# Differential attention in two groups of heads, with value and output projection pieces between its units

## The chip, the cores and the metric

The kernel runs on one core of a Trainium2 chip. A core has five engines with a queue each: TensorE (PE; its weight loads are shown apart as PEld), VectorE (DVE), ScalarE (ACT), GpSimd (POOL, not used here) and SyncE (SP, which here only issues transfers). The metric is the device time of one launch in microseconds. Lower is better.

## What is computed

Two transformer blocks of 2 layers each over 256 tokens of width 1024, all in float32. Each layer is a gated feed-forward, a mixer and a second gated feed-forward. Layer 1 of the first block has the mixer that the change touches, differential attention:

```python
def diff_attention_mixer(h, w_in, w_out, qk_g, lam_p, subln_g, cos, sin, lambda_init):
    q, k, v = jnp.split(h @ w_in, 3, axis=-1)          # 8 heads, 2 maps of 64 each; v: 8 heads of 128
    q = partial_rope(rmsnorm(q, qk_g[0]), cos, sin)
    k = partial_rope(rmsnorm(k, qk_g[1]), cos, sin)
    lam = exp(sum(lp[0] * lp[1])) - exp(sum(lp[2] * lp[3])) + lambda_init
    ...                                                # per block of 128 queries, causal keys
        p = jax.nn.softmax(jnp.where(mask, sc, -jnp.inf), axis=-1)
        a = p[:, :, 0] - lam * p[:, :, 1]
        outs.append(jnp.einsum('bhqk,bhkv->bhqv', a, v[:, :, :s1]))
    o = rmsnorm(concatenate(outs), subln_g) * (1.0 - lambda_init)
    return o.transpose(0, 2, 1, 3).reshape(Bn, S, D_MODEL) @ w_out
```

## The kernel before

Every engine's instruction stream is written out by hand, with semaphores between them, so the order of each queue is the order of the source. A weight matrix is streamed in pieces of 128 by 2048 floats through a ring of three buffers. SP loads a piece into `raw` as soon as DVE has released the buffer. ACT rounds it to `wH` (`cut`, L514), DVE subtracts to get `wL` (`cut`, L897), and PE multiplies three times for each product (`times_three`, L1599, L1601 and L1603) so that the sum has float32 accuracy. ACT may cut piece n once PE has eaten piece n-3. A piece of 512 output columns and half of the depth takes 24 multiplications, 12 for each of the two tiles of 128 tokens.

The mixer uses 16 pieces: two each for six chunks of 512 columns (chunks 0 and 1 queries, 2 and 3 keys, 4 and 5 values), then four for the output projection. Products go to four PSUM banks `PY` (the first two are `PA`, the last two `PB`) and two banks `GU` in turn; `TM` takes transposes. For chunks 0 to 3 ACT squares the bank (L751), DVE normalizes and rotates, PE transposes (`turn_chunk`) and ACT copies the result to `qT` or `kT` (L757). The two value chunks are copied to `vB` by ACT (L665). Ahead of all this DVE works out lambda and the angles (`lambda_and_angles`, L1255 to L1275) in front of the cut of the first piece of the loop.

Attention then runs in 8 units of two heads and one tile of 128 queries; units 0 to 3 are tile 0 (128 keys, "small" below), units 4 to 7 tile 1 (256 keys, "large"). For unit u:

- PE `scores(u)` (L1909) into `PB` for even u and `PA` for odd u, so the scores of u+2 are issued ahead of the rest of unit u;
- DVE `mask_and_max(u)` (L1282), ACT `exponentials(u)` (L733), DVE `difference(u)` (L1293 to L1302). DVE's queue holds mask(u+1) ahead of difference(u);
- PE `turn_weights(u)` (L1918), ACT `weights_out(u)` (L739), PE attention times values into `GU` (L1948; "AV" below).

After units 3 and 7, `out_norm` normalizes all 8 heads of one tile (ACT square L656 and root L660, DVE L1099 to L1104, then a second DVE pass, L1541, with the norm weight). Only after unit 7 does PE transpose the whole result (L1957) into `PY`, ACT and DVE split it in four banks (L728, L1248), and PE runs the four projection pieces. The third kind of mixer (`nsa`, layers 2 and 3) has units of its own through the same `scores` and `mask_and_max`, with one pair of banks and a whole piece in each unit; there DVE's queue holds the weights of unit u (`gated`) ahead of mask(u+1).

Of the kernel before, what the change touches and what calls it, by code (L numbers as in the profile page):

```python
# [25 lines left out]
P = 128  # L26
S = 256
# [38 lines left out]
N_LATE = 6  # L66
# [9 lines left out]
PIECES_B = whole([h * 512 for h in range(6)]) + whole([3 * D + h * 512 for h in range(2)])  # L76
# [39 lines left out]
def build(nc, T, out, upto=99):  # L116

    with ExitStack() as ctx:
# [34 lines left out]
        vec = sb("vec", [P, P + 4 * MODS + 64])  # L153
        cols, bT, peT = vec[:, 0:P], vec[:, P:P + 4 * MODS], vec[:, P + 4 * MODS:]
# [87 lines left out]
        PBf = PY[:, 2:4, :].rearrange("p b n -> p (b n)")  # L242
        TMf = TM[:, :, :].rearrange("p b n -> p (b n)")
# [66 lines left out]
        s_sv = sem("s_sv")  # L310
        s_yb = sem("s_yb")
# [37 lines left out]
        def _(sp):  # L349
# [81 lines left out]
            def late_constants():  # L431
# [3 lines left out]
                for to, name in ((vb[:, :], "a_onorm"), (vb2[:, 0:P], "b_qk_g"), (vb2[:, P:2 * P], "b_subln"),  # L435
# [70 lines left out]
        def _(act):  # L506
# [218 lines left out]
            def high_bank(b):  # L725

                act.wait_ge(s_ot, t.next(s_ot))
                act.activation(xH2[:, b, :], PY[:, b, :], ACT.Copy).then_inc(s_xh, 1)  # L728
# [12 lines left out]
            def diff():  # L741
# [6 lines left out]
                for c in range(4):  # L748
                    banks = GUf if c % 2 == 0 else PAf
                    act.wait_ge(s_eaten, t.next("done", 2))  # L750
                    act.activation(sq_, banks, ACT.Square).then_inc(s_sq, 1)  # L751
# [4 lines left out]
                    dst = (qT if c < 2 else kT)[:, 4 * (c % 2):4 * (c % 2) + 4, :].rearrange("p h s -> p (h s)")  # L756
                    act.activation(dst, TMf, ACT.Copy).then_inc(s_aT, 1)  # L757
                evacuate(vB[:, :, 0:512], GU[:, :, :])
                cut()
                exponentials(0, P)  # L760
                evacuate(vB[:, :, 512:D], PY[:, 0:2, :])
                cut()
                for u in range(8):
                    if u < 7:
                        exponentials(u + 1, P * ((u + 1) // 4 + 1))
                    weights_out(u, S * (u // 4 + 1))
# [5 lines left out]
                for b in range(4):  # L772
                    high_bank(b)
                cut()
                cut()
# [109 lines left out]
        def _(dve):  # L885
# [164 lines left out]
            def ffn(l, j):  # L1050
# [25 lines left out]
                loop(NF - 3, turns > 0)  # L1076
                gate_columns(l, j)
# [18 lines left out]
            def head_norm(src, groups, width, spread, sq):  # L1096
# [7 lines left out]
                chained(dve.tensor_tensor(spread, src, bc(st8[:, 3, 0:groups].unsqueeze(2), [P, groups, width]),  # L1104
                                          ALU.mult))
# [140 lines left out]
            def low_bank(b):  # L1246
                dve.wait_ge(s_xh, t.next(s_xh))
                dve.tensor_tensor(xL2[:, b, :], PY[:, b, :], xH2[:, b, :], ALU.subtract).then_inc(s_xl, 1)  # L1248

            def lambda_and_angles():  # L1250
# [6 lines left out]
                chained(dve.tensor_scalar(vb2[:, P:2 * P], vb2[:, P:2 * P], 1.0 - LAMBDA_INIT, None, ALU.mult))  # L1257
# [14 lines left out]
                dve.tensor_scalar(flat, flat, -3.1415925, 3.1415925, ALU.max, ALU.min).then_inc(s_trig, 1)  # L1272
                dve.wait_ge(s_trigd, 1)
# [3 lines left out]
            def mask_and_max(u, tile, banks):  # L1277

                dve.wait_ge(s_score, t.next(s_score))
                src, dst, width = banks.rearrange("p (m s) -> p m s", s=S), p_[u % 2], P * (tile + 1)  # L1280
                for m in range(4):
                    ins = dve.tensor_tensor_reduce(dst[:, m, 0:width], src[:, m, 0:width],  # L1282
# [33 lines left out]
            def diff():  # L1316
                lambda_and_angles()
                cut()
                q16 = qk_.rearrange("p (g n) -> p g n", n=64)
                q4 = qk_.rearrange("p (t g n) -> p t g n", t=NT, n=64)  # L1320
                shape = [P, NT, 8, 8]
                for c in range(4):
                    banks = GUf if c % 2 == 0 else PAf
# [892 lines left out]
```

## Time and profile before

| | |
|---|---|
| median of 3 runs | 2291.11 us (2289.98 to 2291.81) |
| profiled execution, own time | 2292.84 us |
| its span in the profile | 2291.1 us |
| PE busy | 2181.4 us, 95% of the span |
| DVE busy | 1627.5 us, 71% |
| ACT busy | 1062.4 us, 46% |
| mean granted clock of PE | 0.985 |

The span is the time from the first to the last recorded instruction; busy times are sums of instruction durations. A PE multiplication's own duration includes the time to drain, so the distance from one start to the next is the better price of one in a run.

### The profile page before, as it was taken

Reading aid. Unit: us, or ns where it says so; the run is one execution under the profiler, and the core shown is the slowest. Engines: PE = TensorE matmul, PEld = TensorE weight load, DVE = VectorE, ACT = ScalarE, POOL = GpSimd, SP = SyncE. Lnnn points to the kernel's source line nnn. Section 1 sums busy time; section 2 is a strip of 40 time slices with the busy share of each in tenths; the row PEclk is TensorE's granted clock in tenths of the full one; section 3 lists DMA queues with packets and bytes.
Section 4 is the critical chain, followed back from the end, with each engine's and each line's share of the span. In section 5 each row is a group of like instructions: output and inputs, shape, how many; then the busy total and the mean of one; then the engine's idle time right before and its main releaser. Section 6 shows DMA issues by size and latency. Waiting matters only on the chain.

```text
span 2291.1 us, 29525 instructions
## 1 busy us (share of the span) xinstructions
PE 2181.4 (95%) x10588; PEld 1803.3 (79%) x10588; DVE 1627.5 (71%) x2262; ACT 1062.4 (46%) x1265; POOL 0.2 (0%) x4
## 2 busy tenths in 40 slices
PE   3999989999999996999999999999999999999998
PEld 2888987788788874788788887778878888777887
DVE  6777767777777786677677766577767776656545
ACT  3344533443534455533443446653344344665334
POOL 0000000000000000000000000000000000000000
PEclk9999999999999997999999999999999999999999
DMA  7898524688688641498678853359867885334553
GB/s 308 315 336 318 214 85 153 233 316 312 230 326 315 225 171 59 162 336 299 217 277 310 317 211 129 131 186 341 296 216 282 307 316 212 129 129 147 191 194 129
DMA packets 128372, 537.25 MB, mean 234 GB/s; under 512 B 15040, under 2 KB 15904, under 8 KB 109344
## 3 DMA queue, kind: packets, MB, share of 16 engines
q1 hardware_dynamic: 128288, 536.12, 64.5%
q8 instruction: 55, 0.90, 0.2%
q14 instruction: 29, 0.24, 0.0%
HBM read 534.96 MB, written 1.10 MB: 234 GB/s over the span
## 4 chain that ended last, share of the span: by engine, by line
PE 86%; DVE 8%; ACT 4%; DMA 1%; issue 1%; SPq 0%; DVEq 0%; ACTq 0%
PE GU L1599 14%; PE GU L1603 14%; PE GU L1601 14%; PE PY L1599 11%; PE PY L1601 11%; PE PY L1603 11%; DVE wL L897 3%; PE TM L1643 1%; ACT wH L514 1%; ACT M L566 1%; PE PY L2006 1%; ACT xH L561 1%; PE PY L1909 1%; DMA M<-in_ada_t 1%; PE TM L1799 1%
## 5 line engine op out<-in xcount | busy, mean ns | idle before, releaser
L897 DVE TENSOR_TENSOR wL<-raw,wH 128x2048 fp32r<-128x2048 f32 x344 | 776.7, 2278 | 231.7 <-ACT wH L514 230.6
L514 ACT ACTIVATE wH<-raw 128x2048 fp32r<-128x2048 f32 x344 | 645.3, 1900 | 156.9 <-PE PY L1603 93.2
L1599 PE MATMUL GU<-wH,xH 128*128 128x512 f32 (+1 forms) x1584 | 627.6, 396 | 34.2 <-DVE xL L1021 30.7
L1603 PE MATMUL GU<-wH,xL 128*128 128x512 f32 (+1 forms) x1584 | 616.1, 389 | 0.0
L1601 PE MATMUL GU<-wL,xH 128*128 128x512 f32 (+1 forms) x1584 | 615.0, 388 | 0.0
L1599 PEld LDWEIGHTS GU<-wH,xH 128*128 128x128 f32 x1584 | 298.2, 188 | 100.4 <-issue 27.6
L1603 PEld LDWEIGHTS GU<-wH,xL 128*128 128x128 f32 x1584 | 297.9, 188 | 62.7
L1601 PEld LDWEIGHTS GU<-wL,xH 128*128 128x128 f32 x1584 | 298.5, 188 | 57.1
L594 ACT ACTIVATE hH<-TM 128x512 fp32r<-128x512 f32 x80 | 47.9, 599 | 592.2 <-PE TM L1643 592.2
L910 DVE CUSTOM_DVE_ANT_0 ada<-ada,cond 128x1024 f32<-128x1024 f32 x272 | 316.7, 1221 | 0.0
L1599 PE MATMUL PY<-wH,hH 128*128 128x512 f32 x640 | 198.6, 392 | 0.9 <-DVE wL L897 0.9
L1034 DVE TENSOR_TENSOR hL<-TM,hH 128x512 fp32r<-128x512 f32 x80 | 55.3, 692 | 200.0 <-ACT hH L594 199.4
L1601 PE MATMUL PY<-wL,hH 128*128 128x512 f32 x640 | 197.2, 389 | 0.0
L1603 PE MATMUL PY<-wH,hL 128*128 128x512 f32 x640 | 197.1, 389 | 0.0
L1599 PE MATMUL PY<-wH,xH 128*128 128x512 f32 x448 | 182.1, 406 | 9.4 <-ACT ada L842 3.0
L1601 PE MATMUL PY<-wL,xH 128*128 128x512 f32 x448 | 177.1, 395 | 0.0
L1603 PE MATMUL PY<-wH,xL 128*128 128x512 f32 x448 | 176.7, 394 | 0.0
L1599 PEld LDWEIGHTS PY<-wH,hH 128*128 128x128 f32 x640 | 119.0, 188 | 27.3 <-DVE wL L897 3.4
L1601 PEld LDWEIGHTS PY<-wL,hH 128*128 128x128 f32 x640 | 120.1, 188 | 25.2
L1603 PEld LDWEIGHTS PY<-wH,hL 128*128 128x128 f32 x640 | 120.1, 188 | 25.1
L1599 PEld LDWEIGHTS PY<-wH,xH 128*128 128x128 f32 x448 | 85.7, 191 | 30.0 <-DVE wL L897 4.3
L1603 PEld LDWEIGHTS PY<-wH,xL 128*128 128x128 f32 x448 | 85.6, 191 | 18.9
(282 smaller groups left out, 1899.8 us busy)
## 6 DMA issues: line engine op xcount, KB each, us to landing
raw<-in_up_w SPq DMA_DIRECT2D x352, 512.0 KB, 6.0
ada<-in_ada_t SPq DMA_DIRECT2D x136, 1024.0 KB, 7.8
raw<-in_down_w SPq DMA_DIRECT2D x176, 512.0 KB, 4.7
raw<-in_c_w SPq DMA_DIRECT2D x96, 512.0 KB, 4.3
raw<-in_a_w SPq DMA_DIRECT2D x40, 512.0 KB, 4.4
raw<-in_b_w SPq DMA_DIRECT2D x32, 512.0 KB, 4.3
M<-in_ada_t SPq DMA_DIRECT2D x8, 1024.0 KB, 12.4
gB<-gates SPq DMA_DIRECT2D x12, 512.0 KB, 5.8
```

Source lines behind the costliest of these rows:

```text
L514: act.activation(wH[:, to, 0:words], raw[:, slot, 0:words], ACT.Copy).then_inc(s_high, 1)
L561: act.activation(xH[:, 2 * b:2 * b + 2, toks], modf[:, i, 2 * b:2 * b + 2, :], ACT.Copy).then_inc(s_xh, 1)
L566: ins = act.activation(modf[:, i, d, :], PT[:, i, d, :], ACT.Identity, bias=mod[:, m + d:m + d + 1], scale=scl[:, d:d + 1])
L594: act.activation(hH[:, :, :].rearrange("p f s -> p (f s)"), TM[:, 0, :], ACT.Copy).then_inc(s_hh, 1)
L897: dve.tensor_tensor(wL[:, to, 0:words], raw[:, slot, 0:words], wH[:, to, 0:words], ALU.subtract).then_inc(s_split, 1)
L910: ins = dve.tensor_tensor_reduce(w, w, cond[:, :], 1.0, 0.0, ALU.mult, ALU.add, acc[:, 2 * q + b:2 * q + b + 1])
L1034: dve.tensor_tensor(hL[:, :, :].rearrange("p f s -> p (f s)"), TM[:, 0, :], hH[:, :, :].rearrange("p f s -> p (f s)"), ALU.subtract).then_ ...
L1599: pe.matmul(outs[i], aH, wh[i], start=first, stop=False)
L1601: pe.matmul(outs[i], aH, wl[i], start=False, stop=False)
L1603: ins = pe.matmul(outs[i], aL, wh[i], start=False, stop=last)
L1643: ins = pe.transpose(TM[:, 0, f * S + i * P:f * S + (i + 1) * P], sh[:, 1, i, f * P:(f + 1) * P], ident)
L1799: ins = pe.matmul(dst[:, h, :], kk[:, h, :], qq[:, h, :], start=True, stop=True)
```

## The change

The mixer is reordered.

1. The pieces come as chunks q 0-3, k 0-3, q 4-7, k 4-7, v, v. The units take heads 0 to 3 first (units 0 to 3), then heads 4 to 7; tile 0 and tile 1 alternate. Unit 0's scores are issued between the two pieces of the first value chunk.
2. The second value chunk has no place of its own ahead of the units: units 0 to 3 each hold 12 multiplications of 256 columns, units 4 and 5 hold 24 of them each.
3. All scores go to `PB` alone. `scores(u+1)` is issued at the head of unit u, behind AV of unit u-1.
4. `out_norm` works on a group of four heads for both tiles. Its multiplication with the norm weight is gone: the weight, as a column, is the scale of ACT's and DVE's split. Group 0 is copied out of `GU` by ACT first. Unit 6 holds the transposes of group 0, unit 7 the first projection piece; the second follows unit 7; then come the transposes of group 1 and the last two pieces.
5. `lambda_and_angles` moves into the feed-forward before the mixer, behind its loop. What needs the exponentials (`lambda_last`) stays, behind the cut.
6. One constant fewer is loaded late, and the table of columns is 16 columns wider.

```diff
-PIECES_B = whole([h * 512 for h in range(6)]) + whole([3 * D + h * 512 for h in range(2)])
+PIECES_B = whole([h * 512 for h in (0, 2, 1, 3, 4, 5)]) + [
+    (k0, 3 * D + h * 512, 512) for k0 in (0, 4) for h in range(2)]
...
+            def high_group(grp):
                 act.wait_ge(s_ot, t.next(s_ot))
+                act.activation(xH[:, 4 * grp:4 * grp + 4, :].rearrange("p (b d) s -> p b (d s)", d=2),
+                               TM[:, :, :] if grp else PAb, ACT.Identity, scale=subln).then_inc(s_xh, 1)
...
             def diff():   # ACT
                     cut()
                     cut()
+                    if c == 3:
+                        exponentials(0, P)
                     act.wait_ge(s_ot, t.next(s_ot))
...
                 evacuate(vB[:, :, 0:512], GU[:, :, :])
                 cut()
-                exponentials(0, P)
-                evacuate(vB[:, :, 512:D], PY[:, 0:2, :])
-                cut()
                 for u in range(8):
                     if u == 4:
                         head_norm(GUf, xn[:, 0, :])
+                        act.activation(on_[0], GUf, ACT.Copy).then_inc(s_readA, 1)
+                    if u < 7:
+                        exponentials(u + 1, P * ((u + 1) % 2 + 1))
+                    weights_out(u, S * (u % 2 + 1))
+                    if u == 3:
+                        act.wait_ge(s_half, 1)
+                        act.activation(vB[:, :, 512:768], PAb[:, :, 0:256], ACT.Copy).then_inc(s_readA, 1)
+                    if u == 4:
                         head_root(8)
+                    if u == 5:
+                        evacuate(vB[:, :, 768:D], PAb[:, :, 256:512])
+                        cut()
+                    if u == 6:
+                        high_group(0)
+                        cut()
+                root_table()
                 head_norm(GUf, xn[:, 0, :])
                 head_root(8)
+                cut()
+                high_group(1)
...
             def diff():   # DVE
-                lambda_and_angles()
-                cut()
+                cut()
+                lambda_last()
...
                 for u in range(8):
                     if u < 7:
                         if u:
                             dve.wait_ge(s_a, t.next(s_a))
-                        mask_and_max(u + 1, (u + 1) // 4, PBf if u % 2 else PAf)
-                    difference(u, u // 4)
+                        mask_and_max(u + 1, (u + 1) % 2, PBb)
+                    difference(u, u % 2)
                     if u == 0:
                         cut()
                     if u == 4:
                         out_norm(0)
+                    if u == 5:
+                        cut()
+                    if u == 6:
+                        low_group(0)
+                        cut()
                 out_norm(1)
+                cut()
+                low_group(1)
...
             def diff():   # PE
                 for u in range(8):
+                    tile, first = u % 2, 4 * (u // 4)
+                    if u < 7:
+                        following(u + 1)
+                    if u == 0:
+                        pe.wait_ge(s_aT, t.next(s_aT))
                     turn_weights(u, tile, 2)
+                    if u < 4:
+                        ...
+                        ins = value_half(0, u // 2, u % 2)
+                    elif u < 6:
+                        ...
+                        value_half(1, u - 4, 0)
+                        value_half(1, u - 4, 1).then_inc(s_eaten, 1)
+                    elif u == 6:
+                        pe.wait_ge(s_readA, t.next(s_readA))
+                        pe.wait_ge(s_on, t.next(s_on))
+                        for h in range(4):
+                            for i in range(NT):
+                                ins = pe.transpose(...)
+                        ins.then_inc(s_ot, 1)
+                    else:
+                        pe.wait_ge(s_scored, t.next(s_scored))
+                        pe.wait_ge(s_xl, t.next(s_xl))
+                        project(0, 0)
                     pe.wait_ge(s_aT, t.next(s_aT))
                     ...
+                project(0, 1)
+                pe.wait_ge(s_on, t.next(s_on))
+                ...
+                project_last(1)
```

`value_half(part, q, i)` multiplies tile i with columns 256*part to 256*part+255 of the second value chunk over half q of the depth, 12 multiplications into `PA`.

## Rows read from the trace of the kernel before

**Rows 1.** The page, granted clock of PE in 40 equal slices, tenths of full speed.
```profile
PEclk9999999999999997999999999999999999999999
```
**Rows 2.** Windows: length, busy (count) of PE, PEld, DVE, ACT, POOL; clock; DMA; GB/s.
```profile
862.00:868.80 6.80, 6.80 (x35) 5.04 (x33) 2.25 (x10) 1.77 (x9) 0.00 (x0) 1.00 0.53 192
868.80:921.80 53.00, 30.15 (x145) 22.61 (x144) 35.66 (x126) 29.20 (x78) 0.00 (x0) 0.65 0.06 20
921.80:943.90 22.10, 22.07 (x98) 18.30 (x99) 11.59 (x13) 8.43 (x10) 0.00 (x0) 1.00 0.67 242
```
**Rows 3.** Windows, stretches of the units and of the tail behind them.
```profile
882.90:889.80 6.90, 4.44 (x30) 2.85 (x29) 6.30 (x30) 4.85 (x18) 0.00 (x0) 1.00 0.01 2
889.80:893.20 3.40, 0.43 (x4) 0.19 (x2) 1.36 (x2) 2.79 (x3) 0.00 (x0) 1.00 0.00 0
893.20:910.20 17.00, 12.33 (x50) 9.98 (x51) 11.38 (x40) 7.37 (x21) 0.00 (x0) 0.50 0.00 1
...
917.00:920.50 3.50, 3.42 (x16) 3.02 (x15) 1.65 (x3) 1.84 (x4) 0.00 (x0) 0.50 0.00 0
```
**Rows 4.** Timeline around the first chunks: start, duration, engine, line, operation, count [idle before].
```profile
804.75 0.50 PE L1599 MATMUL PY<-wH,xH 128*128 128x512 f32 x1
...
813.16 0.50 PE L1599 MATMUL PY<-wH,xH 128*128 128x512 f32 x1 [2.64 <-DVE wL L897]
...
820.37 1.03 PE L1974 MATMUL TM<-cst,M 128*128 128x128 f32 x8
...
833.22 0.48 PE L1599 MATMUL PY<-wH,xH 128*128 128x512 f32 x1
...
844.22 1.03 PE L1974 MATMUL TM<-cst,M 128*128 128x128 f32 x8
...
853.32 4.49 DVE L897 TENSOR_TENSOR wL<-raw,wH 128x2048 fp32r<-128x2048 f32 x2
```
**Rows 5.** Timeline, links of the units: L1282 mask, L1918 transposes, L1948 AV, L1909 scores.
```profile
875.47 0.28 DVE L1282 CUSTOM_DVE_ANT_0 M<-PY,cst 128x128 f32<-128x128 f32 x1
...
878.17 0.69 PE L1918 MATMUL TM<-cst,M 128*128 128x128 f32 x2 [1.23 <-DVE M L1302]
...
882.72 0.42 DVE L1282 CUSTOM_DVE_ANT_0 M<-PY,cst 128x256 f32<-128x256 f32 x1 [1.93 <-PE PY L1909]
...
883.59 0.71 PE L1948 MATMUL GU<-M 128*128 128x128 f32 x4 [0.47 <-ACT M L739]
...
884.24 1.13 PE L1909 MATMUL PY<-M 64*128 64x256 f32 x8
...
885.93 0.43 DVE L1282 CUSTOM_DVE_ANT_0 M<-PY,cst 128x256 f32<-128x256 f32 x1
...
885.95 0.44 PE L1918 MATMUL TM<-cst,M 128*128 128x128 f32 x2 [0.58 <-DVE M L1302]
...
889.57 0.66 PE L1918 MATMUL TM<-cst,M 128*128 128x128 f32 x4 [0.93 <-DVE M L1302]
```
**Rows 6.** Timeline, AV of a large unit and the scores behind it.
```profile
895.08 2.08 PE L1948 MATMUL GU<-M 128*128 128x128 f32 x8 [4.85 <-DVEq L1540]
...
897.09 2.08 PE L1909 MATMUL PY<-M 64*128 64x256 f32 x8
```
**Rows 7.** Timeline, small scores in the third mixer's units.
```profile
1427.46 0.72 PE L1909 MATMUL PY<-M 64*128 64x128 f32 x8
```
**Rows 8.** Chain of work: start, duration, a multiplication of 256 columns in the first mixer.
```profile
250.10 0.12 PE PY L1760
```
**Rows 9.** The page, cuts of a piece: shapes, count, busy, mean ns, idle before.
```profile
L897 DVE TENSOR_TENSOR wL<-raw,wH 128x2048 fp32r<-128x2048 f32 x344 | 776.7, 2278 | 231.7 <-ACT wH L514 230.6
L514 ACT ACTIVATE wH<-raw 128x2048 fp32r<-128x2048 f32 x344 | 645.3, 1900 | 156.9 <-PE PY L1603 93.2
```
**Rows 10.** Timeline, a copy of two banks (ACT) and a norm's multiplication (DVE).
```profile
868.86 1.02 ACT L665 ACTIVATE M<-PY 128x1024 f32<-128x1024 f32 x1 [2.83 <-PE PY L1603]
...
893.75 1.23 DVE L1104 TENSOR_TENSOR M<-GU,st 128x1024 f32<-128x1024 f32 x1
```

More of the change, by code:

```diff
@@ L748, in diff @@
                 for c in range(4):
-                    banks = GUf if c % 2 == 0 else PAf
                     act.wait_ge(s_eaten, t.next("done", 2))
-                    act.activation(sq_, banks, ACT.Square).then_inc(s_sq, 1)
+                    act.activation(sq_.rearrange("p (b n) -> p b n", b=2), PAb if c % 2 else GU[:, :, :],
+                                   ACT.Square).then_inc(s_sq, 1)
                     head_root(16)
@@ L1076, in ffn @@
                 loop(NF - 3, turns > 0)
+                if (l, j) == (1, 0):
+                    lambda_and_angles()
                 gate_columns(l, j)
@@ L1336, in diff @@
                 t.next(s_ot)
-                cut()
-                mask_and_max(0, 0, PBf)
+                mask_and_max(0, 0, PBb)
                 for u in range(8):
@@ L1348, in diff @@
                         out_norm(0)
+                    if u == 5:
[3 more added lines that the diff above has]
+                        cut()
                 out_norm(1)
-                for b in range(4):
-                    low_bank(b)
+                cut()
+                low_group(1)
                 t.next(s_at, 2)
-                t.next(s_ot, 4)
+                t.next(s_ot, 2)
                 t.next(s_on, 6)
-                t.next(s_readA, 2)
-                cut()
-                cut()
+                t.next(s_readA)
             def keys_rotated(src, branch):
@@ L1899, in hgrn, with scores @@
                 project_last(1)
-            def scores(u, tile, keys, heads, queries=qT, double=True):
-                banks = (PAf if double and u % 2 else PBf).rearrange("p (m s) -> p m s", s=S)
-                if u > double:
+            def scores(u, tile, keys, heads, queries, banks):
+                if u:
                     pe.wait_ge(s_scored, t.next(s_scored))
@@ L1924, in diff @@
                 keys = lambda h: kT[:, h, :]
-                heads = lambda u: (2 * (u % 4), 2 * (u % 4) + 1)
-                for c in range(1, 6):
+                heads = lambda u: (u // 2 * 2, u // 2 * 2 + 1)
+                following = lambda u: scores(u, u % 2, keys, heads(u), qT, PBb)
+                for c in range(1, 5):
                     if c > 1:
@@ L1929, in diff @@
                     for q in range(2):
-                        if c == 5 and q == 1:
-                            pe.wait_ge(s_aT, t.next(s_aT))
-                            scores(0, 0, keys, heads(0))
+                        if c == 4 and q == 1:
+                            following(0)
                         by_token(B if c % 2 else A, q)
                     turn_chunk(c - 1)
-                pe.wait_ge(s_readA, t.next(s_readA, 2))
-                scores(1, 0, keys, heads(1))
-                for u in range(8):
-                    tile = u // 4
-                    if u < 6:
-                        scores(u + 2, (u + 2) // 4, keys, heads(u + 2))
+                slots = [t.next("piece") % RING for _ in range(2)]
@@ new lines, in value_half @@
+                def value_half(part, q, i):
+                    cols_v = slice(part * S, (part + 1) * S)
+                    for k in range(4):
+                        d = 4 * q + k
+                        a, b = slice(i * P, (i + 1) * P), slice(k * 512 + part * S, k * 512 + (part + 1) * S)
+                        ins = times_three([B[i][:, cols_v]], xH[:, d, a], xL[:, d, a], [wH[:, slots[q], b]],
+                                          [wL[:, slots[q], b]], d == 0, d == ND - 1)
+                    return ins
@@ L1951, in diff @@
                         ins.then_inc(s_o, 1)
[L1952 to L1955 removed]
+                project(0, 1)
+                pe.wait_ge(s_on, t.next(s_on))
+                for h in range(4):
                     for i in range(NT):
[L1957 to L1963 removed]
+                        ins = pe.transpose(TMf[:, h * S + i * P:h * S + (i + 1) * P],
+                                           on_[1][:, i * 512 + h * P:i * 512 + (h + 1) * P], ident)
+                ins.then_inc(s_ot, 1)
+                pe.wait_ge(s_xl, t.next(s_xl))
+                project_last(1)
             def turn_chunk(c):
@@ L2042, in nsa @@
                 pairs = lambda u: (u // 2 % 2 * 2, u // 2 % 2 * 2 + 1)
-                following = lambda u: scores(u, u // 4, keys(u), pairs(u), qT2, False)
+                following = lambda u: scores(u, u // 4, keys(u), pairs(u), qT2, PY[:, 2:4, :])
                 following(0)
```

102 lines of the change are left out of this document (53 added, 49 removed).

## The prediction

> **What bounds the kernel now.** I read the page first, then windows by stage, then the timeline of the mixer with its waits. PE is busy 95% of the span, and the granted clock has one dent of note, in the slice of this mixer [rows 1]. The windows show why: the mixer's projections before and behind attention run PE without a gap at full clock, but the 53.0 us of attention between them keep it busy for 30.15 us at a mean clock of 0.65 [rows 2]. There PE waits in turn for DVE and ACT: the units are a chain through three engines, not a PE load. A second, smaller hole lies ahead: before the second piece of chunk 1 PE stands 2.64 us because DVE cuts that piece only behind lambda and the angles [rows 4]. So there are two things to win: the hole, and work of PE put into attention's idle time.
>
> **How the clock goes.** In the units the clock stayed at full speed for 882.9 to 889.8 with PE busy 4.44 of 6.90 us, was at half behind the 3.40 us with 0.43 us of work, stayed at half through 17.00 us in which PE was busy for 12.33 with short gaps, and came back only behind 3.42 of 3.50 us without a gap [rows 3]. At half, large scores take 2.08 us against 1.13, AV of a large unit 2.01 from start to start [rows 5, 6]; I take a factor of 1.93 for PE's work.
>
> **Part 1, lambda and angles moved.** The first chunk behind the hole took 820.37 - 804.75 = 15.62 us to its transposes, an undisturbed one 844.22 - 833.22 = 11.00 [rows 4]. The difference, 4.6 us, is the wait and the half-clock stretch that it caused; it goes. In the feed-forward the same small operations take 3.9 us of DVE (an estimate from the timeline: they fill DVE from the end of the cut before 804.75 on). A turn of that loop has three cuts of 2.28 us [rows 9] and lasts about 17 us of PE, so DVE has the room; the tightest piece I find is ready with it, and I charge 0 to 0.5 us, and take 0. Next late is PE's own load: the transposes of chunk 0 then wait for nothing. Gain 4.6, bounds 4.1 and 4.6.
>
> **Part 2, the unit's chain.** This is the term that decides. Before, scores(u+2) are in the other banks ahead of time, and DVE goes from one unit to the next without a pause (mask 882.72, next mask 885.93 [rows 5]). Now scores(u+1) wait for the AV of unit u-1, and in DVE's queue mask(u+1) stands ahead of difference(u). So transposes(u) need difference(u), which needs mask(u+1), which needs scores(u+1): one line, with PE idle for all of DVE's part. The links at full clock:
> - scores to mask start: 1.13 + 0.1 = 1.2 large [rows 5], 0.72 + 0.1 = 0.8 small [rows 7];
> - mask start to transposes: 878.17 - 875.47 = 2.70 small behind small, 885.95 - 882.72 = 3.23 large mask and small difference, 889.57 - 885.93 = 3.64 both large [rows 5]; a small mask and large difference is 2.70 + 3.64 - 3.23 = 3.1;
> - transposes 0.3 (small) or 0.6 (large) to the next start [rows 5]; 12 multiplications of 256 columns at 0.12 = 1.44 [rows 8];
> - AV 884.24 - 883.59 = 0.65 small [rows 5], half of 2.01 = 1.0 large [rows 6].
>
> ACT's copy of the weights hides under the 1.44 us. A small unit is 1.2 + 3.2 + 0.3 + 1.44 + 0.65 = 6.8 us, a large one 0.8 + 3.1 + 0.6 + 1.44 + 1.0 = 6.95.
>
> The 96 multiplications of 256 columns replace 48 of 512 at 0.227: 11.5 us for 10.9, a loss of 0.6 that is inside these terms. The Trainium skill ("TensorE: Matmul & The Clock Gate", LDWEIGHTS) prices a load of 128 columns at 107 ns, as long as 256 columns stream; were it not hidden, the 96 would cost some 10 us more by an estimate from that page. The row shows 0.12 us with a load for each, so it is hidden, and the sum is unchanged.
>
> **Part 3, the schedule at full clock**, in times of the trace before:
> - chunk 3's transposes start 11.8 behind 844.22, less 4.6, plus 0.7 of scores(0): 852.1, ended at 853.1 [rows 4]. Mask(0) stands behind two cuts, which end at 857.8 - 4.6 = 853.2 [rows 4]. Scores(1) start at 854.2.
> - Unit 0: DVE is done at 858.6, transposes and values at 860.4. But ACT has exponentials(0) (1.7), two copies of 1.0 [rows 10], a cut of 1.9 [rows 9] and exponentials(1) (2.0) ahead of the weights: AV(0) ends at 862.9.
> - Units 1 to 3: 6.95 + 6.8 + 6.95: 883.6.
> - Unit 4: as a small unit but 2.88 of values: 8.25, 891.9; ACT's square and copy and DVE's norm hide under it. Unit 5: 8.4, 900.3.
> - Unit 6 is the first pile-up. ACT copies the last values only when unit 5's piece is eaten, then cuts (0.6 + 1.9); DVE's cut of that piece (2.2) stands ahead of mask(7). Mask starts at 899.3 + 4.9 = 904.2, transposes(6) at 907.4; eight more transposes and AV: 909.2.
> - Unit 7 is the second: high half 1.0, cut 1.9, DVE's cut 2.2 and difference(7) 2.0 stand in one line behind the transposes of group 0 (908.6): 916.0. Then 0.6, a piece of 5.45, AV 1.0: 923.1.
> - Tail: square, sums, root, multiplication are 1.0 + 1.4 + 0.3 + 1.5, less than the piece beside them (928.5); transposes 0.9, high 1.2, low 1.3 (both of two banks): 931.9, and 10.9 for the last pieces: 942.8.
>
> Before, the last projection ends at 943.9 [rows 2]. So at full clock everywhere the change gives 1.1 us, with the 4.6 of part 1 in it. What the two moved value pieces and two moved output pieces save (21.8 us) is paid back by a chain 26 us longer. The second DVE pass of the norm (1.23, as [rows 10]) and the last wait for four separate banks are gone in these figures.
>
> **Part 4, the clock.** In a unit PE works 3.6 us and then stands 3.2 to 3.4 in one piece; in the pile-ups 6 us. That is nearer to the stretch of rows 3 behind which the clock was at half than to 4.44 of 6.90. The unbroken runs are 3.6 us, 7 at half, so it will also come back. PE's work on the chain from 853 to 932, without the two output pieces, is 8 scores and AV (12.9), transposes (5.3) and values (11.5) = 29.7 us. All at half adds 0.93 x 29.7 = 27.6; none adds 0. Of the 53 us before, about 70% were at half [rows 2]; in the third mixer's units, filled by whole pieces, none [rows 1]. I take half: +13.8. "A second HAM failure mode: psum-queue depth-cycling" on the same page of the Trainium skill describes such gaps as making the clock go back and forth; by that rule too the moved work would not be had at full rate, and the trace agrees (0.65).
>
> **Sum.** -1.1 + 13.8 = +12.7 on the profiled execution's 2292.84: 2305.5. That execution lies 1.7 us over the median shown, so 2303.8; I say 2304. What follows is the same feed-forward with the same transfers, whose buffers come free earlier; at nothing.
>
> **Rivals.**
> - *The clock holds.* The pieces between the units keep it at full, as in the third mixer. For it: 882.9 to 889.8 held with 64% busy. Against: there the gaps were short, and here each unit has one over 3 us, as the third mixer (weights of unit u ahead of mask(u+1)) has not. Time: 2291.1 - 1.1 + 0 to 3 = 2291.5. Chance 0.12.
> - *Faster: DVE does not hold up the last units.* If the cuts beside units 5 to 7 were through before mask(7) and difference(7) are due, the first pile-up gives back 4.7 us (mask at 901.5 less the wait) and the second 6, and with them 4 us of clock: 2304 - 15 = 2289. It needs ACT's cut of piece 13 to be ended by 899; the source has it behind the copy of the last values. Chance 0.05.
> - *Clock at half for nearly all of it*, as behind 893.2 [rows 3]: -1.1 + 25 = 2315. Against: the runs of 5.8 us at half in each unit have no gap, those of rows 3 had. Chance 0.10.
> - *The change does less than it says:* lambda's block delays the feed-forward's cuts by its 3.9 us and the gain of part 1 is lost: forecast + 4 = 2308. Chance 0.05.
>
> **Numbers.** The forecast as sized holds 0.68. A measurement of this kernel tells 0.2%, 4.6 us, from no change. Slower by more: forecast, half clock, lost gain and little of the first rival, 0.82. Within: most of the first rival and the low edge of the forecast, 0.11. Faster: 0.07. The range runs from 2291 (clock holds) to 2312 (three quarters at half, 2304 + 7).
>
> **What would show it.** Right: the hole before 813 is gone and the first transposes come 4.6 us earlier; scores of unit u+1 begin only behind AV of u-1; PE waits some 3.2 us for DVE's difference in each unit, a period of about 7 us at full and 10 at half clock; waits near 6 us before the transposes of units 6 and 7 that end in DVE's difference behind a cut; clock under 1 in about half of 853 to 932; last projection near 956. Wrong: transposes that wait for nothing (then DVE's queue isn't the link), a clock of 1.00 through the units, or time lost outside this mixer.

## The result, and the profile after

The changed kernel takes 2307.28 us (median of 4 runs, 2306.09 to 2308.90), the kernel before 2291.03 (4 runs, 2289.98 to 2291.81): a ratio of 1.0069 with a 95% interval of 1.0057 to 1.0082. The change makes the kernel 16 us slower. Its profiled execution took 2306.38 us with a span of 2304.6, which is 13.5 us over the 2292.84 of before's; the readings below say where those 13.5 lie. The other 2.7 come from how far each profiled execution lies from its own median: before's 1.8 us above, the changed one's 0.9 below.

The page of the changed kernel, in 40 slices of 57.6 us. PEclk is the granted clock in tenths:

```profile
PE   3999989999999995899999999999999999999998
...
PEclk9999999999999997899999999999999999999999
```

The dent of [rows 1] is still one slice, with a shallow second one behind it, and PE's load has its dent there (5 and 8 tenths). The loss is in this mixer. The start of a stage can be read from the first projection that waits for its normed input. In the timeline of PE, first in the kernel before, the start of this mixer:

```profile
791.03 0.47 PE L1599 MATMUL GU<-wH,xH 128*128 128x512 f32 x1 [1.43 <-DVE xL L1021]
```

and the same in the changed kernel:

```profile
792.89 0.47 PE L1627 MATMUL GU<-wH,xH 128*128 128x512 f32 x1 [1.43 <-DVE xL L1036]
```

The same row at the other boundaries gives a table of stage lengths, in us, from one such row to the next. It is used for every kernel below, each from its profiled execution:

| kernel | feed-forward ahead (1,0) | this mixer | feed-forward behind (1,2) |
|---|---|---|---|
| before | 191.93 | 156.08 | 193.02 |
| changed | 193.68 | 166.42 | 192.88 |

So 10.3 us were lost in the mixer and 1.8 in the feed-forward ahead of it, to which lambda's block has moved. That is 12.1 of the 13.5; the other 1.4 lie behind 1140 us, in code that is the same in both.

PE's waits in the kernel before from 790 to 945 (us in total, times, longest) are a mixed list. Its first lines:

```profile
PE PY L1957 <- DVE M L1541: 5.8, 1, 5.8
PE TM L1918 <- DVE M L1302: 5.8, 5, 2.3
PE GU L1948 <- DVEq L1540: 4.9, 1, 4.9
PE GU L1948 <- ACT M L739: 4.0, 7, 0.7
```

In the changed kernel, from 850 to 965, one line stands out:

```profile
PE TM L1944 <- DVE M L1324: 32.3, 8, 6.4
PE PY L1627 <- DVE xL L1265: 2.5, 1, 2.5
```

One wait, in each of the eight units: the transposes of the weights (L1944) for the difference (L1324). The same in the timeline, with units 1, 2, 3, 6 and 7 and the idle time before each in brackets:

```profile
869.08 1.11 PE L1944 MATMUL TM<-cst,M 128*128 128x128 f32 x4 [3.27 <-DVE M L1324]
878.02 0.44 PE L1944 MATMUL TM<-cst,M 128*128 128x128 f32 x2 [3.39 <-DVE M L1324]
885.55 0.66 PE L1944 MATMUL TM<-cst,M 128*128 128x128 f32 x4 [3.26 <-DVE M L1324]
...
915.10 0.69 PE L1944 MATMUL TM<-cst,M 128*128 128x128 f32 x2 [5.95 <-DVE M L1324]
924.75 1.11 PE L1944 MATMUL TM<-cst,M 128*128 128x128 f32 x4 [6.39 <-DVE M L1324]
943.31 0.50 PE L1627 MATMUL PY<-wH,xH 128*128 128x512 f32 x1 [2.52 <-DVE xL L1265]
```

There are two sizes of gap: 3.3 us in a plain unit, 6 us in the last two. The two transposes of a small unit take 0.44 us in some units and 0.69 in others, which is the clock. The windows of the changed kernel (columns: us, then busy time of PE, PEld, DVE, ACT and POOL, the granted clock, the DMA share and GB/s), first units 0 to 6, then two stretches at half clock, the second of which reaches into unit 7:

```profile
855.70:923.50 67.80, 36.65 (x220) 32.70 (x220) 32.48 (x118) 32.09 (x84) 0.00 (x0) 0.77 0.15 54
...
858.80:865.60 6.80, 5.28 (x26) 4.81 (x26) 3.50 (x6) 4.59 (x11) 0.00 (x0) 0.50 0.26 74
...
913.40:930.50 17.10, 9.00 (x30) 7.64 (x31) 6.93 (x15) 7.46 (x14) 0.00 (x0) 0.50 0.42 150
```

Against [rows 2], PE has more work in this part (the moved value and output pieces), and no engine is busy for more than 55% of it.

The time at half clock is not what changed. In both kernels it adds up to 40.9 us of the mixer: before in three stretches (814.7 to 818.1 behind the hole, 872.7 to 882.9, 893.2 to 920.5), in the changed kernel in seven (six between 858.8 and 930.5, and 944.1 to 947.5). PE is busy for 27.5 us of it before and for 30.8 in the changed kernel.

### The profile page after: what moved, and what is told of

Read it like the earlier page. It is cut to its first block, busy times and chain, and to the rows that moved or that the text cites. A ratio compares the mean times of both kernels' runs of the same rounds, so it can differ in the third digit from the quotient of the medians.

```text
span 2304.6 us, 29619 instructions
## 1 busy us (share of the span) xinstructions
PE 2184.7 (95%) x10636; PEld 1811.2 (79%) x10636; DVE 1624.0 (70%) x2258; ACT 1063.7 (46%) x1266; POOL 0.2 (0%) x4
## 4 chain that ended last, share of the span: by engine, by line
PE 86%; DVE 8%; ACT 3%; DMA 1%; issue 1%; SPq 0%; DVEq 0%; ACTq 0%
PE GU L1627 14%; PE GU L1631 14%; PE GU L1629 14%; PE PY L1627 11%; PE PY L1629 11%; PE PY L1631 11%; DVE wL L912 3%; PE TM L1671 1%; ACT wH L518 1%; PE PY L2066 1%; PE PY L1935 1%; ACT M L570 1%; ACT xH L565 1%; DMA M<-in_ada_t 1%; PE PY L1638 1%
## 5 line engine op out<-in xcount | busy, mean ns | idle before, releaser
L1627 PEld LDWEIGHTS GU<-wH,xH 128*128 128x128 f32 x1584 | 298.2, 188 | 100.4 <-issue 27.4
L1627 PE MATMUL PY<-wH,xH 128*128 128x512 f32 (+1 forms) x464 | 189.8, 409 | 7.9 <-ACT ada L857 3.0
L1629 PE MATMUL PY<-wL,xH 128*128 128x512 f32 (+1 forms) x464 | 184.0, 397 | 0.0
L1631 PE MATMUL PY<-wH,xL 128*128 128x512 f32 (+1 forms) x464 | 183.5, 396 | 0.0
L1627 PEld LDWEIGHTS PY<-wH,hH 128*128 128x128 f32 x640 | 118.9, 188 | 27.5 <-DVE wL L912 3.3
L1627 PEld LDWEIGHTS PY<-wH,xH 128*128 128x128 f32 x464 | 92.4, 199 | 27.6 <-issue 4.2
L1631 PEld LDWEIGHTS PY<-wH,xL 128*128 128x128 f32 x464 | 92.3, 199 | 18.7
```

Of the source, the lines that this page charges most:

```text
L1627: pe.matmul(outs[i], aH, wh[i], start=first, stop=False)
L1629: pe.matmul(outs[i], aH, wl[i], start=False, stop=False)
L1631: ins = pe.matmul(outs[i], aL, wh[i], start=False, stop=last)
```

## The experiments

Twelve kernels ran, in four groups (e1 to e4, e5 to e8, e9 to e11, e12), each group on one chip with the kernel before beside it (medians there 2291.5, 2291.9, 2290.9 and 2290.9). The changed kernel's 2307.28 comes from a run of its own, so differences of medians against it are across groups. The ratio is worked out from the single executions and not from the two medians. The stage lengths are those of one execution each; that of e7 lies 3.0 us above e7's median, e8's 2.5, e11's 1.8, e4's 1.6, the others' within 1.3. Where an expectation speaks of filler matmuls of 256 columns, they were in fact of 512, about 0.24 us each: the operand `xH[:, 4:6, :]` has 2 x 256 columns.

| run | median us | ratio to before (95%) | feed-forward ahead | mixer |
|---|---|---|---|---|
| e1 block in the feed-forward, late | 2291.85 | 1.0002 (0.9994 to 1.0011) | 196.49 | 151.21 |
| e2 block ahead of its loop | 2292.94 | 1.0000 (0.9991 to 1.0009) | 194.49 | 151.20 |
| e3 changed + fillers | 2296.70 | 1.0018 (1.0009 to 1.0028) | 196.60 | 155.94 |
| e4 changed + queue order | 2297.07 | 1.0022 (1.0013 to 1.0031) | 196.91 | 156.44 |
| e5 changed + cuts moved | 2302.58 | 1.0048 (1.0036 to 1.0060) | 197.09 | 160.43 |
| e12 changed, block on GpSimd | 2304.34 | 1.0057 (1.0045 to 1.0069) | 191.87 | 166.41 |
| e10 order, cuts, GpSimd | 2284.93 | 0.9981 (0.9970 to 0.9992) | 191.92 | 149.44 |
| e9 the same, half fillers | 2284.14 | 0.9969 (0.9958 to 0.9980) | 191.92 | 148.28 |
| e6 the same, full fillers | 2288.09 | 0.9984 (0.9975 to 0.9993) | 191.98 | 152.65 |
| e7 before, block on GpSimd | 2288.32 | 0.9981 (0.9973 to 0.9990) | 191.99 | 152.93 |
| e8 the same, full fillers | 2293.40 | 1.0005 (0.9997 to 1.0014) | 192.03 | 158.16 |
| e11 the same, half fillers | 2283.77 | 0.9968 (0.9956 to 0.9980) | 191.94 | 149.14 |

**Part 1 alone: the block's place.** Both are the kernel before with lambda's and the angles' block moved, e1 to the place that the change gives it, e2 ahead of the feed-forward's loop:

```diff
             def diff():
-                lambda_and_angles()
                 cut()
+                lambda_last()
...
+                if (l, j) == (1, 0):
+                    lambda_and_angles()
                 gate_columns(l, j)
```

> The kernel before with part 1 of the change alone (lambda and angles behind the loop of the feed-forward ahead of the mixer). Theory: the hole before chunk 1 is worth 4.6 us, but in the trace of the changed kernel the mixer starts 1.75 us later, because the 3.9 us block holds back a cut, the buffer's transfer and then ACT. So 2.9 us faster, 2288.1, and the same 1.3 us wait before the last transposes of that feed-forward. Rival (the prediction's sum, block hidden): 4.6 us faster, 2286.4.

> The kernel before with the same block ahead of that loop instead of behind it. Theory: each turn of the loop leaves DVE some us free, so the lag is made up long before the end; the hole's 4.6 us come in full: 2286.4, mixer starting within 0.3 us of the kernel before. Rival (the later start of the mixer in the changed kernel is chance, or the block's own 3.9 us anywhere): as e1_lam_late.

Neither gained. e1 gave less than either side of its expectation; e2 came out like e1, as its rival says. The mixer is shorter by 4.9 us in both, about the 4.6 forecast, and the feed-forward longer by 4.6 and 2.6. In e1 the feed-forward has a stretch of 3.4 us at half clock near its end; e3 to e5 have one too, the changed kernel, with the same block in the same place, has none in its profiled execution and is only 1.8 us longer there. What it is paid with can be seen on DVE in the changed kernel. The block's last operation, and the cut behind it:

```profile
748.99 0.18 DVE L1292 TENSOR_SCALAR ang<-ang 128x32 f32<-128x32 f32 x1
...
749.22 2.28 DVE L912 TENSOR_TENSOR wL<-raw,wH 128x2048 fp32r<-128x2048 f32 x1
```

In the kernel before that cut began 4.0 us earlier:

```profile
745.23 2.29 DVE L897 TENSOR_TENSOR wL<-raw,wH 128x2048 fp32r<-128x2048 f32 x1
```

PE does not wait for this cut. But its raw buffer comes free 4 us later (the next transfer is issued at 754.56 for 750.57 before), and later transfers shift with it. Some 26 us on, ACT waits for a transfer with a cut that stands in its queue ahead of its part of `sh`. Before, and then in the changed kernel:

```profile
772.77 1.92 ACT L514 ACTIVATE wH<-raw 128x2048 fp32r<-128x2048 f32 x1 [1.21 <-DMA raw<-in_b_w]
774.60 0.36 ACT L602 ACTIVATE sh<-GU 128x256 f32<-128x256 f32 x1
```

```profile
775.34 1.92 ACT L518 ACTIVATE wH<-raw 128x2048 fp32r<-128x2048 f32 x1 [3.38 <-DMA raw<-in_b_w]
777.16 0.36 ACT L606 ACTIVATE sh<-GU 128x256 f32<-128x256 f32 x1
```

DVE finishes `sh` behind it, and PE, which turns it, waits. This wait is in the changed kernel's list from 600 to 791; the kernel before has none there:

```profile
PE TM L1707 <- DVE sh L1055: 1.3, 1, 1.3
```

In e2 the waits are at the loop's start instead, for the cuts themselves (1.6 and 0.6 us, from the same list of e2):

```profile
PE PY L1603 <- DVE wL L897: 1.6, 1, 1.6
PE GU L1603 <- DVE wL L897: 0.6, 1, 0.6
```

**The clock's share.** e3 puts matmuls on data that is there into the gaps, ahead of each unit's transposes; the bank is overwritten by them:

```diff
+                    for _ in range([12, 11, 13, 11, 13, 11, 24, 26][u]):
+                        pe.matmul(TM[:, u % 2, :], xH[:, 4, 0:P], xH[:, 4:6, :].rearrange("p d s -> p (d s)"),
+                                  start=True, stop=True)
                     turn_weights(u, tile, 2)
```

> The changed kernel with multiplications of no use (12, 11, 13, 11, 13, 11, 24, 26 of 512 columns, into the transposes' bank) ahead of the transposes of units 0 to 7, in PE's wait for DVE. Theory clock: about 13 us of the units' chain is PE work at half clock; with no gap the granted clock stays at 1.00 from 853 to 932 and the kernel gets 11 to 14 us faster, 2295, although PE does 27 us more. Rival chain only: the clock is no cost of its own, then at best nothing changes, and where a filler outlasts the wait it adds some us: 2307 to 2315.

Windows of e3 over the units, columns as above:

```profile
853.40:921.20 67.80, 61.89 (x373) 50.45 (x372) 36.34 (x129) 34.13 (x87) 0.00 (x0) 1.00 0.25 86
```

The clock stays at 1.00 where it was at 0.77, and the mixer is 10.5 us shorter, although nothing was done to any wait and PE is busy for 25 us more. By medians it is 10.6 us faster than the changed kernel, a little short of the 11 to 14 expected. The fillers hardly stand in the way: in units 1 to 7 PE still waits 0.2 to 0.9 us for the difference behind them, and only the transposes of unit 0 come later than in the changed kernel, by 1.2 us from the start of the mixer. So half clock costs the changed kernel 10.5 to some 12 us.

**The queue order.** e4 gives the changed kernel the order of the third mixer on DVE and ACT:

```diff
+                    difference(u, u % 2)
                     if u < 7:
                         if u:
                             dve.wait_ge(s_a, t.next(s_a))
                         mask_and_max(u + 1, (u + 1) % 2, PBb)
-                    difference(u, u % 2)
...
+                    weights_out(u, S * (u % 2 + 1))
                     if u < 7:
                         exponentials(u + 1, P * ((u + 1) % 2 + 1))
-                    weights_out(u, S * (u % 2 + 1))
```

> The changed kernel with difference(u) ahead of mask(u+1) in DVE's queue and the weights' copy ahead of the exponentials of u+1 in ACT's, as the third mixer has it. Theory queue order: the transposes no longer wait for mask(u+1) and the scores before it; a unit's period falls from about 7 (full) or 9 to 10 (half) us to 5.3 us and the clock falls less often: 12 to 14 us faster than the changed kernel, 2294. Rival single bank of scores: what binds is that scores(u+1) wait behind AV(u-1), whatever DVE's order: under 4 us gained, 2303 or more.

The mixer is 10.0 us shorter and the median 10.2, where 12 to 14 were expected. The list of waits of e4 from 840 to 960:

```profile
PE TM L1944 <- DVE M L1324: 24.0, 6, 7.5
```

Two of the eight waits are gone and 8.3 of the 32.3 us; the longest is the last one, for a difference behind a cut, and it is longer than before (7.5 for 6.4). So the order of the queues was a link of the chain. e4 moved an operation on DVE and one on ACT together; which of them gave how much isn't shown, only that PE's wait was for DVE's difference. Little of it came by the clock: that was at half for 34.1 us of e4's units, for 37.5 in the changed kernel's. The longest wait left is behind a cut, which e5 tests.

**The pile-ups.** e5 leaves the order as the change has it and moves two cuts:

```diff
                     if u == 5:
+                        cut()
                         evacuate(vB[:, :, 768:D], PAb[:, :, 256:512])
-                        cut()
...
                     if u == 6:
                         low_group(0)
+                    if u == 7:
                         cut()
                 out_norm(1)
```

> The changed kernel, with two weight cuts moved: ScalarE's cut of piece 13 stands ahead of the copy of the last value banks in unit 5 (in the changed kernel behind it), and VectorE's cut of piece 14 stands behind difference(7) instead of ahead of it. Theory (the two pile-ups of the prediction cost time of their own: mask(7) behind copy, cut and cut in unit 5, difference(7) behind low half and cut in unit 6): about 4 to 8 us come back, 2299 to 2303 us. Rival (the pile-ups lie beside other work, or the clock takes back what they give): 2306 to 2308 us, as the change. If only the clock mattered, removing a wait would leave TensorE's half-speed stretches and give about half of it, 2304 to 2305.

The waits of units 6 and 7, 5.95 and 6.39 us above, are plain ones in e5:

```profile
914.14 0.44 PE L1945 MATMUL TM<-cst,M 128*128 128x128 f32 x2 [3.39 <-DVE M L1324]
920.32 1.12 PE L1945 MATMUL TM<-cst,M 128*128 128x128 f32 x4 [3.59 <-DVE M L1324]
```

The two are 5.4 us shorter together, and the mixer is 6.0 us shorter. By medians the kernel gains 4.7 us, within the 4 to 8 expected (in the profiled executions its feed-forward is 3.4 us longer than the changed kernel's).

**The block on an idle engine.** In e12 GpSimd does the block during the first layer (sums of 64 by six halvings, and the fused multiply-add as two operations); the rest is the changed kernel. e7 is the same on the kernel before.

```diff
+        @block.gpsimd
+        def _(pool):
...
+            pool.wait_ge(s_late, N_LATE * 16)
+            lambda_and_angles()
```

> The changed kernel with only the lambda and angle block taken from VectorE's feed-forward and done by GpSimd in the first layer; the units, their queues and the cuts as the change has them. Theory (the block costs 1.8 us of the feed-forward in the change's profiled execution, up to 5 in e3 to e5, and the units' 166 us are as they were): 2302 to 2305 us, 2 to 5 under the change, the feed-forward back at 191.9 to 192.0 us and the mixer at 164 to 167. Rival (the whole of the change's loss lies in the block's place): 2288 to 2292.

> The kernel before, with only the lambda and angle block taken off VectorE and done by GpSimd, which is otherwise idle, during the first layer. Runs e1 and e2 showed the mixer 4.9 us shorter without the block on VectorE ahead of its cuts, and the feed-forward 2.6 to 4.6 us longer with it. Theory (the block costs where VectorE's cuts feed TensorE, wherever it stands on VectorE): nothing is paid, 2286 to 2287 us. Rival (GpSimd's instructions hold VectorE up, or what the mixer gains is lost in the wait for the next weights): 2289 to 2292 us.

In both the feed-forward is at 191.9 us again; e12 keeps the 166.4 of the changed mixer, and is 2.9 us under the changed kernel by medians (the intervals of the two ratios overlap, so the size is uncertain). e7 gains 3.6, between its theory and its rival. Its mixer is 152.93 where e1 had 151.2: the low-clock stretches in its units last 44.4 us for 37.5 in e1, in the same instructions.

**Everything together, and the same for the kernel before.** e6, e9 and e10 are the changed kernel with the edits of e4, e5 and e12, and with full, half and no fillers. e8 and e11 are e7 with full and half fillers.

```diff
+                    for _ in range([7, 6, 6, 6, 6, 6, 8, 8][u]):
+                        pe.matmul(TM[:, u % 2, :], xH[:, 4, 0:P], xH[:, 4:6, :].rearrange("p d s -> p (d s)"),
+                                  start=True, stop=True)
                     turn_weights(u, tile, 2)
```

That is e9; e6 has 14, 11, 12, 11, 12, 11, 16, 16 and e10 none. In the kernel before, e11 (e8 in brackets) has 8, 4, 3, 3, 4, 3, 3, 3 (14, 8, 4, 4, 8, 8, 8, 8) at the same place and two more groups:

```diff
                     if u == 4:
+                        for _ in range(18):
+                            pe.matmul(TM[:, 1, :], xH[:, 4, 0:P], xH[:, 4:6, :].rearrange("p d s -> p (d s)"), start=True, stop=True)
                         pe.wait_ge(s_readD, t.next(s_readD))
...
                 t.next(s_scored, 2)
+                for _ in range(22):
+                    pe.matmul(TM[:, 0, :], xH[:, 4, 0:P], xH[:, 4:6, :].rearrange("p d s -> p (d s)"), start=True, stop=True)
                 pe.wait_ge(s_readD, t.next(s_readD))
```

> The changed kernel with everything at once that the first four runs and the theory point to: difference(u) ahead of mask(u+1), weights out ahead of the exponentials, the two cuts moved as in e5, the lambda and angle block taken off VectorE and done by GpSimd during the first layer (the same arithmetic; sums of 64 by halving), and filler matmuls on data that is there, with their result overwritten, ahead of each unit's transposes (14, 11, 12, 11, 12, 11, 16, 16 of 256 columns). Theory: filler alone gave 2296.7; the queue order and the cuts at full clock should take some 7 us more, the block on the idle engine 2 to 4: 2284 to 2288 us, faster than the kernel before by 3 to 7. Rival (filler took all that the order gives, the gaps being the same ones): 2292 to 2295 us, no faster than the kernel before.

> The kernel before with the block on GpSimd as in e7, and filler matmuls of 256 columns where TensorE waits in its units: 14, 8, 4, 4, 8, 8, 8, 8 ahead of the units' transposes, 36 ahead of the weighted sum of unit 4, and 44 ahead of the last transposes of the normed output. Theory (the clock is what costs the kernel before too, some 37 us of its mixer at half speed with TensorE some two thirds busy): another 5 to 10 us from e7, 2277 to 2282 us. Rival (at full clock the units wait for VectorE and ScalarE instead, and little is gained): 2284 to 2287 us. If fillers stand in the way: above e7.

> As e6_all_fill with the fillers halved: 7, 6, 6, 6, 6, 6, 8, 8 ahead of the units' transposes. (The fillers of e3, e6 and e8 were matmuls of 512 columns, 0.24 us each in their traces, and not of 256: those of e6 took 2.8 to 3.9 us a unit, and TensorE did not wait for VectorE at all in its units 1 to 4, so the fillers themselves stood in the way there.) Theory: the waits come back at some 1 us a unit, the clock still holds, and 1 to 4 us are gained on e6: 2284 to 2287 us. Rival (half the filler doesn't hold the clock): 2290 to 2293.

> As e6_all_fill without any filler: queue order, the two cuts, the block on GpSimd. Theory (queue order, cuts and filler all take from the same idle time of TensorE, and the clock falls again where the units' waits are left): 2290 to 2293 us, above e6. Rival (the order alone keeps TensorE busy enough; filler adds nothing then): 2285 to 2288.

> As e8_before_pool_fill with the fillers about halved (8, 4, 3, 3, 4, 3, 3, 3 ahead of the transposes, 18 ahead of the weighted sum of unit 4, 22 ahead of the last transposes), so that by 0.23 us each they fit into the waits of 4.85 and 5.77 us. Theory (e8 was slower than e7 since its fillers were twice as long as the waits that they filled): 2283 to 2287 us, faster than e7's 2288.3. Rival (the large units of this kernel run at VectorE's 3.6 us whatever the clock, so the clock is worth nothing here): 2288 to 2290 us, as e7.

e10, without a filler, is already 22.4 us under the changed kernel and 6.0 under the one before; its mixer is 17.0 us shorter than the change's, about what e4 and e5 gave one by one (16.0). This is the rival's side of its expectation (2285 to 2288). PE still waits 19.8 us for differences in its units, 6.2 at the longest. Windows over its units, and over those of e9 behind it:

```profile
855.00:905.00 50.00, 31.76 (x213) 28.84 (x213) 30.50 (x116) 28.93 (x76) 0.00 (x0) 0.81 0.16 51
```

```profile
855.00:904.00 49.00, 39.05 (x267) 32.61 (x268) 30.86 (x117) 29.00 (x76) 0.00 (x0) 0.98 0.17 54
```

Fillers that fit raise the clock from 0.81 to 0.98 and bring the mixer 1.2 us more, which by the medians (0.8) and the ratios, whose intervals overlap, can't be told from nothing. Fillers that don't fit cost more than the clock gives: e6's took 2.8 to 3.9 us a unit, and its mixer is 3.2 us longer than e10's; e8 is 5.1 us over e7, where 5 to 10 less were expected. The other expectations held: e6 at the slow edge of its theory, e9, e11 and e12 within theirs. With fillers that fit, the kernel before gains too: e11's mixer is 3.8 us shorter than e7's. The clock over about the same part was 0.65 in the kernel before [rows 2] and 0.57 in e7 (864 to 916); in e11:

```profile
860.00:912.00 52.00, 40.44 (x221) 29.93 (x220) 35.21 (x126) 29.18 (x78) 0.00 (x0) 0.93 0.07 21
```

e9 and e11 are the fastest kernels of this study, 6.8 and 7.2 us under the kernel before in their group, and not apart from each other. So the new layout with its queues and cuts mended is worth as much as the old one, 148.28 us for 149.14, and not more. Neither is free of waits (the longest before the transposes in e9 is 4.3 us), and the old layout was not tried with its queues reordered.

## Why the prediction was right, and where its terms were off

The forecast was 2304 us, slower, in 2291 to 2312; measured were 2307.28. In the profiled execution it was +12.7 for a measured +13.5. That it came so near is luck in part: the mixer's term was 2.4 us too high, and 3.2 us came from places that the sum had at nothing. By medians the difference is 16.3 us.

**Part 1 (gain 4.6, charge 0 to 0.5): the gain right, the charge mis-sized.** e1 and e2 measured the gain at 4.9 us, and in the changed kernel the first transposes come 24.7 us behind the start of the mixer instead of 29.3. The charge was 1.8 us in the changed kernel's profiled execution, 2.9 by the medians of e12 against it, and 2.6 to 5.2 in e1 to e5. The step that failed was "DVE has the room; the tightest piece I find is ready with it". PE's wait for the delayed cut was looked at; what was not is the buffer that the cut frees, the transfer into it and ACT's queue behind that transfer. The rival "lambda's block delays the feed-forward's cuts by its 3.9 us and the gain of part 1 is lost" is what e1 and e2 show (ratios 1.0002 and 1.0000), and its chance of 0.05 was too low.

**Part 2 (a unit is one chain): right.** Waits of 3.2 us for the difference in each unit were forecast, and 3.26 to 3.39 are in the trace. A unit's period was to be about 7 us at full and 10 at half clock; from the transposes of one unit to those of the next, units 0 to 5 take 8.9, 8.9, 7.5, 9.0 and 7.7 us, all but the last with a stretch at half. e4 shows the link that the part named: with the difference ahead of the mask (and the weights' copy ahead of the exponentials), 10 us come back. The 96 multiplications of 256 columns are at 0.12 us from start to start where the clock is at 1.00, as in rows 8. Their weight loads are recorded at 0.19 us each there and don't show in that distance, so they are hidden, as the prediction took them.

**Part 3 (the schedule at full clock, -1.1): near.** With the clock held by fillers, e3's mixer is 155.94 us for before's 156.08, with the cost of the fillers in unit 0 in it. The side remark that the chain is 26 us longer doesn't follow from its own figures, which give 21.8 + 4.6 - 1.1 = 25.3; the sum doesn't use it. The two pile-ups are in the trace at the places given. The first reads on DVE, in the changed kernel:

```profile
909.66 2.29 DVE L912 TENSOR_TENSOR wL<-raw,wH 128x2048 fp32r<-128x2048 f32 x1 [7.53 <-ACT wH L518]
911.87 0.42 DVE L1304 CUSTOM_DVE_ANT_0 M<-PY,cst 128x256 f32<-128x256 f32 x1
```

DVE has been idle for 7.53 us when ACT's cut comes, and mask(7) stands behind DVE's own. The second:

```profile
918.68 1.28 DVE L1265 SCALAR_TENSOR_TENSOR xL<-PY,vec,xH 128x1024 fp32r<-128x1024 f32 x1 [3.64 <-ACT xH L732]
920.48 2.29 DVE L912 TENSOR_TENSOR wL<-raw,wH 128x2048 fp32r<-128x2048 f32 x1 [0.52 <-ACT wH L518]
922.69 0.17 DVE L1315 RECIPROCAL stu<-stu 128x4 f32<-128x4 f32 x1
```

Only the rival built on them was priced too high: it took 4.7 and 6 us and 4 of clock, 15 in all, and e5 gave 6.0 in the mixer. What lay behind the pile-ups was not free for the whole of their length; a plain wait of 3.4 and 3.6 us stayed.

**Part 4 (half of 29.7 us at half speed, +13.8): right in size.** The six stretches at half clock from 858.8 to 930.5 hold 27.4 us of busy PE. By the prediction's factor of 1.93 that is 27.4 x 0.93 / 1.93 = 13.2 us, and e3 returned 10.5 of them, or some 12 with what its fillers cost in unit 0. Whether the rest is PE's work beside waits that would be there anyway isn't shown. This is the price of half clock inside the changed kernel, not what the change added to it: the kernel before has as much time at half, and with the block on GpSimd fillers brought its mixer 3.8 us (e11 against e7). The Trainium skill ("TensorE: Matmul & The Clock Gate", "A second HAM failure mode: psum-queue depth-cycling") says that idle times between groups of matmuls make the clock go to and fro; the units agree, with six falls of the clock in 72 us and a mean of 1.00 where e3 filled the gaps.

**The sum.** The mixer was forecast at +12.7 and measured at +10.3, the feed-forward at 0 and measured at +1.8; 1.4 us lie behind, outside the code that was changed. The last projection, forecast near 956, starts at 955.71, with the 1.9 us by which the mixer starts later in it. The rival "the clock holds" was ruled out by 0.77, "half nearly throughout" as well.

**What the reordering costs by itself.** The runs let it be split, roughly. With the block on GpSimd in both, the new layout's mixer is 13.5 us longer at the clock as it falls (166.41 in e12, 152.93 in e7). With fillers that hold the clock or nearly do (1.00 and 0.93), and no block in the mixer, it is 6.8 us longer (155.94 in e3, 149.14 in e11). So about half of the cost is the longer chain at full clock, and the other half is that half clock costs the new layout more. Its time at half is the same 40.9 us as before's; that more of PE's work there stands in the chain fits this, and isn't shown by itself. These are differences of single profiled executions, of which e7's was a long one, and good to some 3 us.

## What to carry to other kernels

Work that is put between the steps of a chain through three engines doesn't fill the chain's gaps if each step's order in the queues makes it longer: look for an operation for unit u+1 that stands ahead of one for unit u, and change that order first, which here gave as much (10.2 us) as holding the clock did (10.6). A block that an engine "has room for" is priced by the buffers that it holds back and by who waits for the transfers into them, and here such a small block off the critical path went best to the engine with nothing else to do. When the clock falls between short bursts, useless matmuls show in one run how much it costs; in these runs they paid only where they were shorter than the gap. The granted clock alone doesn't say what it costs: two layouts with about as long at half (40.9 us in the changed kernel's mixer, 44.4 in e7's units) got 10.5 and 3.8 us back from fillers.

## What the runs showed of the hardware that was not expected

- The clock was worth less once the queues were mended: fillers gave 10.6 us with the long waits in place (e3) and 0.8 without (e9 against e10), though the clock rose from 0.81 to 0.98 there. One part of it is that less was left to give: 18.4 us of busy PE at half in e10's units, 27.4 in the changed kernel's. That PE's speed matters less where DVE or ACT is late anyway would explain the rest, and isn't shown.
- The same instructions ran at half clock for 37.5 us in e1's units and 44.4 in e7's, whose mixer began 5 us earlier in the execution, and the mixers differ by 1.7 us. Differences of this size between single profiled executions should not be read as effects of an edit.
- GpSimd did the block in some 19 us (128.15 to 147.24 in e7's trace) where DVE took 3.9: one multiplication of 128x128 took 2.61 us there, and 0.23 in DVE's timeline of the kernel before. Its times are uneven: the same multiplication of 128x16 took 0.25 us twice and then 2.22. Nothing waited for it, and the stages around it were not longer than before.
